# A hand-ordered attention, Hyena and conv-FFN kernel: earlier turns of probabilities, an output's turns between the third and fourth weighing, a net layer one gate tile later, and a few smaller reorderings

## The reference

```python
def first_block(x, ...):
    h = rms_norm(x, norm_in)
    (dq, dk, dv, dgate, cq, ckv, kr, mgate, g_diff, g_mla) = split(h @ w_in)
    # four differential heads: two causal softmaxes each, the second weighted by -lam
    o_diff = causal_multimap_attention(rope(dq), rope(dk), dv, [1, -lam], 64 ** -0.5)
    o_diff = rms_norm(o_diff, diff_subln) * (1 - lambda_init) * silu(dgate)
    # four latent heads: queries and keys from low-rank projections
    q = rms_norm(cq, mla_q_norm) @ w_uq;  kv = rms_norm(ckv, mla_kv_norm) @ w_ukv
    o_mla = causal_multimap_attention([q_nope, rope(q_rope)], [k_nope, rope(kr)], mv, [1], 192 ** -0.5)
    o_mla = o_mla * silu(mgate)
    merged = sigmoid(g_diff) * (o_diff @ w_proj_diff) + sigmoid(g_mla) * (o_mla @ w_proj_mla)
    return rms_norm(x + merged @ w_out, norm_final)

def second_block(x, c, ...):
    sh1, sc1, g1, sh2, sc2, g2 = adaln_params(c, mod_w, mod_b)     # the modulation
    x = x + g1 * hyena_mix(modulate(rmsnorm(x, norm_g[0]), sh1, sc1), p)   # its filter: a net of three
                                                   # small layers with sines, evaluated at all positions
    x = x + g2 * conv_ffn(modulate(rmsnorm(x, norm_g[1]), sh2, sc2), ...)
    return rmsnorm(x, final_g)
```

## Time and profile before

| | |
|---|---|
| time, median of 3 runs | 1042.02 us (1041.53 to 1042.57) |
| the profiled execution's own time | 1041.58 us |
| its span | 1039.4 us |
| PE busy | 1027.0 us (99%), 4886 matmuls |
| DVE busy | 738.0 us (71%) |
| POOL busy | 573.1 us (55%) |
| ACT busy | 413.7 us (40%) |
| mean DMA rate | 132 GB/s |

### The profile page before, as it was taken

One profiled execution on the slowest core, in us unless ns is written; L12 is line 12 of the kernel. 1 busy time (PEld: TensorE's weight loads), 2 busy tenths in 40 slices (PEclk: granted clock), 3 DMA queues, 4 the chain that ended last, 5 costly groups with the idle time before them and its releaser, 6 DMA issues.

```text
span 1039.4 us, 13302 instructions
## 1 busy us (share of the span) xinstructions
PE 1027.0 (99%) x4886; PEld 847.7 (82%) x4886; DVE 738.0 (71%) x1053; ACT 413.7 (40%) x681; POOL 573.1 (55%) x420
## 2 busy tenths in 40 slices
PE   9999999999999999999999999999999999999997
PEld 7889887777878888778888888778888888888886
DVE  7768957756878667994888968686666666671563
ACT  4233646665545244743444342533232223231222
POOL 2896996999410064545544276534655546574542
PEclk9999999999999999999999999999999999999999
DMA  8755364432665722404332223312222322223222
GB/s 343 289 199 201 117 212 148 107 137 92 212 172 198 295 109 81 162 14 108 123 122 81 102 84 145 117 65 98 81 81 81 135 107 81 81 81 128 115 81 81
DMA packets 21996, 136.91 MB, mean 132 GB/s; under 512 B 3973, under 2 KB 4405, under 8 KB 15288
## 3 DMA queue, kind: packets, MB, share of 16 engines
q1 hardware_dynamic: 9360, 94.74, 24.4%
q0 software_dynamic: 8224, 31.73, 9.9%
q10 hardware_dynamic: 4358, 9.72, 2.5%
HBM read 128.83 MB, written 6.31 MB: 130 GB/s over the span
## 4 chain that ended last, share of the span: by engine, by line
PE 83%; POOL 5%; DVE 5%; DMA 4%; ACT 2%; issue 1%; SPq 0%; ACTq 0%; POOLq 0%; DVEq 0%
PE bank L526 70%; PE bank L517 7%; DMA arena<-mod_w_in 4%; POOL arena L1819 2%; PE bank L532 2%; POOL arena L1817 1%; PE bank L787 1%; PE bank L781 1%; DVE ring_parts L2025 1%; DVE arena L2178 1%; DMA ring<-weights_in 1%; PE bank L776 1%; POOL mod_part L1822 0%; PE bank L997 0%; ACT ring_parts L1224 0%
## 5 line engine op out<-in xcount | busy, mean ns | idle before, releaser
L1801 POOL TENSOR_TENSOR ring_parts<-ring,ring_parts 128x1024 fp32r<-128x1024 f32 x101 | 251.6, 2497 | 237.7 <-ACT ring_parts L1224 234.1
L526 PE MATMUL bank<-hT_parts,ring_parts 128*128 128x512 f32 x1344 | 339.0, 393 | 1.2 <-ACT hT_parts L1567 1.2
L1224 ACT ACTIVATE ring_parts<-ring 128x1024 fp32r<-128x1024 f32 (+3 forms) x165 | 168.5, 1031 | 370.2 <-PE bank L526 172.6
L526 PEld LDWEIGHTS bank<-hT_parts,ring_parts 128*128 128x128 f32 x1344 | 249.6, 188 | 54.9 <-ACT hT_parts L1567 2.8
L526 PE MATMUL bank<-ring_parts,arena_parts 128*128 128x512 f32 (+1 forms) x744 | 172.9, 384 | 1.1 <-DVE ring_parts L2025 1.1
L526 PE MATMUL bank<-ring_parts,hT_parts 128*128 128x512 f32 (+2 forms) x676 | 168.3, 377 | 0.0
L526 PEld LDWEIGHTS bank<-ring_parts,arena_parts 128*128 128x128 f32 x744 | 137.4, 188 | 28.9 <-DVE ring_parts L2025 1.3
L526 PE MATMUL bank<-arena_parts,ring_parts 128*128 128x512 f32 x592 | 147.9, 390 | 0.0
L526 PEld LDWEIGHTS bank<-ring_parts,hT_parts 128*128 128x128 f32 x676 | 123.2, 188 | 21.0 <-issue 0.2
L2701 DVE SCALAR_TENSOR_TENSOR arena<-bank,small,arena 128x441 f32<-128x441 f32 (+2 forms) x176 | 122.3, 695 | 21.0 <-DVE arena L2701 1.4
L526 PEld LDWEIGHTS bank<-arena_parts,ring_parts 128*128 128x128 f32 x592 | 111.0, 188 | 24.7 <-DVE arena_parts L2458 2.0
(11 more groups left out here) (246 smaller groups left out, 1124.6 us busy)
## 6 DMA issues: line engine op xcount, KB each, us to landing
ring<-weights_in SPq DMA_DIRECT2D x39, 2048.0 KB, 7.9
arena<-mod_w_in POOLq DMA_DIRECT2D x32, 512.0 KB, 4.1
arena<-mod_w_in POOLq DMA_DIRECT2D x8, 1024.0 KB, 9.2
x_sb<-xT_in SPq DMA_DIRECT2D x4, 512.0 KB, 6.8
ring<-weights_in SPq DMA_DIRECT2D x4, 512.0 KB, 7.5
arena<-x_in SPq DMA_DIRECT2D x4, 512.0 KB, 11.0
mod_spill<-mod_part POOLq DMA_DIRECT2D x16, 128.0 KB, 2.2
arena<-mod_spill POOLq DMA_DIRECT2D x8, 256.0 KB, 4.2
```

The lines of the kernel that those rows point to most:

```text
L526: ins = nc.tensor.matmul(out, l, r, start=start and n == 0, stop=stop and n == len(passes) - 1)
L1224: return nc.scalar.activation(out, in_, ACT.Copy)
L1801: return nc.gpsimd.tensor_tensor(part(low), low, part(high), ALU.subtract)
```

## The change

What it does, in eight places:

1. **Early turns.** The first two turns of unit u's probabilities (`first_turns`) leave `values(u)` and go into `scores(u + 1)`: ahead of the masks in a differential unit, ahead of the third of four tiles in a latent one. In unit 0 the last part of the fill goes there too. Unit 7, which has no scores behind it, keeps its order.
2. **Outputs.** `turn_output(1)` to `turn_output(4)` move from behind the fourth weighing of units 3 to 6 to between the third and the fourth, in banks by a table.
3. **Roots.** The inverse roots of outputs are made one modulation chunk sooner on POOL.
4. **Net.** The second net layer comes behind gate tile 5 instead of 4, on TensorE, DVE and ScalarE; the fifth modulation chunk of DVE comes behind piece 12 instead of 13.
5. **Queries.** The last piece of UQ is split in two on DVE: columns 512 to 767 first, the rest behind two other operations.
6. **Fill 0** is cut otherwise: low parts of its first three pieces ahead of the scores of unit 1.
7. **ScalarE** splits the second piece of mgate behind the first copy of values.
8. **n2.** The first `input_full` of DVE comes ahead of the first `taps_ab`, and the other taps shift by a tile.

In the changed kernel the same code stands 2 to 26 lines further down.

```diff
--- before.py
+++ after.py
@@ -68,5 +68,5 @@
 MOD_EARLY = 3
-MOD_AFTER = (9, 13, 16, 17, 19)
+MOD_AFTER = (9, 12, 16, 17, 19)
 SGD_AFTER = 13
-ROOTS_AFTER = (10, 20, 22, 24, 26)
+ROOTS_AFTER = (10, 19, 21, 23, 25)
 PAUSE_AFTER = 16
@@ -126,3 +126,3 @@
 PIECE = SLOT // 4
-NET_AFTER = (2, 4, 7)
+NET_AFTER = (2, 5, 7)
 PIECES = 4
@@ -420,2 +420,4 @@
         FILL_BANK = (7, 5, 5, 5, 5, 5, 5, 3)
+        OUTPUT_BANK = (6, 1, 1, 1, 1, 6, 6, 6)
+        OUTPUT_AT = {3: 1, 4: 2, 5: 3, 6: 4}
 
@@ -704,3 +706,3 @@
                 for i in ((), (), range(KQ), range(KQ, KQ + KKV))[m]:
-                    take((i + 1) % 4, "lat_low", i + 1)
+                    take((i + 1) % 4, "lat_low", i + 1 + (i >= KQ))
                     turn((i + 1) % 4, [lat[:, t, i * P:(i + 1) * P] for t in range(TT)]).then_inc(sem("lat_turned"), 1)
@@ -724,4 +726,6 @@
                 if m == 0:
-                    pe.wait_ge(sem("piece_low"), FIRST_UQ + KQ)
+                    pe.wait_ge(sem("lat_low"), KQ + 1)
+                    pe.wait_ge(sem("piece_low"), FIRST_UQ + KQ - 1)
                 product3(bank[4 + m][:, 0:256], *pairs, start=False, terms=((0, 1),)).then_inc(sem("latq_done"), 1)
+            pe.wait_ge(sem("piece_low"), FIRST_UQ + KQ)
             for h in range(HEADS):
...
@@ -745,3 +749,3 @@
 
-            def scores(u):
+            def scores(u, between=None):
                 latent, h = u >= HEADS, u % HEADS
@@ -783,3 +787,5 @@
                             ins.then_inc(sem("half_scored"), 1)
-                for a, i in tiles:
+                for n, (a, i) in enumerate(tiles):
+                    if between and n == (2 if latent else 0):
+                        between()
                     out, q, keys = place(a, i)
@@ -790,3 +796,3 @@
 
-            def fill(u, qs=range(PIECES), last=True):
+            def fill(u, qs=range(PIECES), low_qs=range(PIECES)):
 
@@ -807,6 +813,8 @@
                         product3(bank[b], lefts[two], rights[two], start=q == 0, stop=False, terms=((0, 0), (1, 0)))
-                    if not last:
+                    if low_qs:
+                        pe.wait_ge(sem("piece_low"), FIRST_MGATE + low_qs[-1] + 1)
+                        ks = slice(2 * low_qs[0], 2 * low_qs[-1] + 2)
+                        ins = product3(bank[b], lefts[ks], rights[ks], start=False, stop=low_qs[-1] == PIECES - 1, terms=((0, 1),))
+                    if not low_qs or low_qs[-1] < PIECES - 1:
                         return
-                    pe.wait_ge(sem("piece_low"), FIRST_MGATE + 4)
-                    ins = product3(bank[b], lefts, rights, start=False, terms=((0, 1),))
                 else:
@@ -818,11 +826,20 @@
 
-            def values(u, between=None):
-                latent, h = u >= HEADS, u % HEADS
+            def turn_probs(u, i):
+                b = 5 + i % 2
                 p1 = probs1[u % 2]
+                pe.wait_ge(sem("probs_ready"), 4 * u + i + 1)
+                take(b, "pT_out", 4 * u + i + 1)
+                turn(b, [p1[:, OFF[i] + j * P:OFF[i] + (j + 1) * P] for j in range(i + 1)]).then_inc(sem("p_turned"), 1)
 
-                def turn_probs(i):
-                    b = 5 + i % 2
-                    pe.wait_ge(sem("probs_ready"), 4 * u + i + 1)
-                    take(b, "pT_out", 4 * u + i + 1)
-                    turn(b, [p1[:, OFF[i] + j * P:OFF[i] + (j + 1) * P] for j in range(i + 1)]).then_inc(sem("p_turned"), 1)
+            def turn_output(u):
+                pe.wait_ge(sem("o_ready"), u + 1)
+                take(OUTPUT_BANK[u], "oT_out", u + 1)
+                turn(OUTPUT_BANK[u], [o_tok[u % 2][:, m, :] for m in range(TT)]).then_inc(sem("o_turned"), 1)
+
+            def first_turns(u):
+                turn_probs(u, 0)
+                turn_probs(u, 1)
+
+            def values(u, between=None):
+                latent, h = u >= HEADS, u % HEADS
 
@@ -837,4 +854,2 @@
 
-                turn_probs(0)
-                turn_probs(1)
                 if between:
@@ -842,5 +857,5 @@
                 weigh(0)
-                turn_probs(2)
+                turn_probs(u, 2)
                 weigh(1)
-                turn_probs(3)
+                turn_probs(u, 3)
                 if between:
@@ -848,9 +863,6 @@
                 weigh(2)
+                if u in OUTPUT_AT:
+                    turn_output(OUTPUT_AT[u])
                 weigh(3)
 
-            def turn_output(u):
-                pe.wait_ge(sem("o_ready"), u + 1)
-                take(6, "oT_out", u + 1)
-                turn(6, [o_tok[u % 2][:, m, :] for m in range(TT)]).then_inc(sem("o_turned"), 1)
-
             def gate_tile(i, part=None):
@@ -877,3 +889,3 @@
                 if m == TT - 1:
-                    fill(0, range(PIECES - 1), last=False)
+                    fill(0, range(PIECES - 1), ())
                 tokens = slice(m * P, (m + 1) * P)
@@ -882,4 +894,9 @@
                          [two_parts(ukv[1], k, slice(0, 512)) for k in range(KKV)]).then_inc(sem("latk_done"), 1)
-            scores(1)
-            fill(0, (PIECES - 1,))
+            fill(0, (), range(PIECES - 1))
+
+            def rest_and_turns():
+                fill(0, (PIECES - 1,), (PIECES - 1,))
+                first_turns(0)
+
+            scores(1, rest_and_turns)
             values(0)
@@ -887,7 +904,8 @@
             for u in range(1, UNITS - 1):
-                scores(u + 1)
+                scores(u + 1, lambda: first_turns(u))
                 values(u)
-                if u >= 2:
-                    turn_output(u - 2)
+                if u == 2:
+                    turn_output(0)
                 fill(u + 1)
+            first_turns(UNITS - 1)
             values(UNITS - 1, lambda part: gate_tile(0, part))
...
@@ -1405,8 +1423,8 @@
                     wait("subln_ready", 1)
-                nc.scalar.activation(kT[:, u, :], bank[6], ACT.Identity, scale=st(SUBLN))
-                nc.scalar.activation(part(qT[:, u, :]), bank[6], ACT.Identity, scale=st(SUBLN)).then_inc(sem("oT_out"), 1)
+                nc.scalar.activation(kT[:, u, :], bank[OUTPUT_BANK[u]], ACT.Identity, scale=st(SUBLN))
+                nc.scalar.activation(part(qT[:, u, :]), bank[OUTPUT_BANK[u]], ACT.Identity, scale=st(SUBLN)).then_inc(sem("oT_out"), 1)
 
-            for m in range(2):
-                split_high(FIRST_MGATE + m)
+            split_high(FIRST_MGATE)
             mv_out(0)
+            split_high(FIRST_MGATE + 1)
             exps(0, (0,))
@@ -2181,2 +2199,9 @@
                 split_low(FIRST_UQ + k)
+
+            def split_last_uq(s):
+                p = FIRST_UQ + KQ - 1
+                wait("piece_high", p + 1)
+                low, high = piece_parts(p)
+                return V.tensor_tensor(part(low[:, s]), low[:, s], part(high[:, s]), ALU.subtract)
+
             for i in range(KQ + KKV):
@@ -2186,3 +2211,3 @@
                 if i == KQ:
-                    split_low(FIRST_UQ + KQ - 1)
+                    split_last_uq(slice(512, UQ_W)).then_inc(sem("lat_low"), 1)
                 wait("lat_out", i + 2 if i else 1)
@@ -2190,2 +2215,3 @@
                                        op0=ALU.mult, op1=ALU.subtract).then_inc(sem("lat_low"), 1)
+            split_last_uq(slice(0, 512)).then_inc(sem("piece_low"), 1)
             for m in range(TT):
@@ -2608,3 +2634,2 @@
             taps_even(0)
-            taps_ab(0, 0)
             wait("modc_ready", 1)
@@ -2613,6 +2638,6 @@
                 input_full("n2", 0, N2_BANKS, x_low, (k,))
-                if k == 0:
-                    taps_ab(0, 1)
-                if 2 <= k < 6:
-                    taps_cd(0, k - 2)
+                if k in (0, 2):
+                    taps_ab(0, k // 2)
+                if 3 <= k < 7:
+                    taps_cd(0, k - 3)
             add_abs(6)
```

8 lines of the change are left out of this document (4 added, 4 removed).

## The result

The changed kernel takes 1049.59 us (median of 4 runs, 1049.27 to 1050.77) against 1042.23 for the kernel before: ratio 1.0074, 95% interval 1.0061 to 1.0087. The forecast was 1045.1 with a range up to 1047.3, so the side was right and the size was not. The profiled run took 1049.27 us for a span of 1047.3.

The account below looks back on a forecast made before the run. TensorE, busy 99%, was taken as the bound. Gains of 5.0 us against 5.2 lost left 0.2 slower; with 2.9 for the clock, 1042.02 became 1045.1 us, range 1040.3 to 1047.3.

Parts of the forecast that it names:

- Net layer moved behind gate tile 5: Net stage: TensorE stands 5.7 us for ScalarE's late Sin, so the third net layer is 5.2 us late.
- The clock: Behind the net stage's stop TensorE's clock falls to half pace for 5.8 us, a loss of 2.9 us.
- Outputs turned between third and fourth weighing: Head loop, four units: an output's turns fill a 0.30 us stop before the fourth weighing; gain 1.15 us (0 to 1.2).
- the tie at 210.44 and 210.49: Unit 3: TensorE would ask for the output at 210.44, and it would be ready at 210.49.
- The sign that I had named: Head loop: TensorE waiting for probs_ready or o_ready would show the prediction wrong.
- Early turns: Units 1 to 6: masks cover ScalarE's copy between turns and first weighing; 0.42 us a unit, gain 2.5 us.
- The outputs of units 4 to 6: Head loop: turning each output before the fourth weighing removes a stop of 0.30 us a unit.
- UQ split: Last query piece: with 256 columns first, TensorE's wait of 1.10 us shrinks; gain 0.5 us (0.2 to 1.4).
- n2: At 439.92: VectorE's x_sb tile ahead of the tap lets TensorE's turn start 0.65 us sooner (0 to 0.8).
- Unit 0: First weighing: the early turn removes a 0.6 us wait, the third gate piece is 0.3 to 0.4 late; gain 0.2.
- The third rival: Head loop: late probabilities or outputs shrink 2.5 + 1.15 to 0; 1045.9 at full clock, 1048.8 with the fall; chance 0.10.
- the forecast: Net stage stop and fall of the clock behind it: 1045.1 us, chance 0.45.

Follow-up runs that it names:

- mod_back: Changed kernel with only the modulation chunk put back behind piece 13, the net layer left at gate tile 5: 1050.26 us, ratio 1.0077.
- mod_back_sin_first: As mod_back, with ScalarE's Sin of the second net layer also moved ahead of gate tile 6's split and sigmoid: 1041.46 us, ratio 0.9994.
- net_back: Changed kernel with the second net layer and the modulation chunk back at their old places: 1040.50 us, ratio 0.9989.
- outputs_back: Changed kernel with the net stage, GpSimd's roots and all four outputs' turns back at their old places: 1043.01 us, ratio 1.0007.
- outputs_back_new_roots: As outputs_back, but with GpSimd's roots at their new, sooner chunks: 1040.77 us, ratio 0.9989.
- net_back_u3: As net_back, with output 1 (unit 3's) turned behind the fourth weighing again: 1041.08 us, ratio 0.9994.
- pool_steps_aside: As net_back, with GpSimd held once, behind modulation chunk 22, until output 1 is ready: 1046.19 us, ratio 1.0039.
- aside_and_row: As pool_steps_aside, with GpSimd requesting the row of inverse roots ahead of its last modulation chunk: 1043.20 us, ratio 1.0008.

## Why the prediction was wrong

- **Net layer moved behind gate tile 5**: right. Stop 5.64 against 5.7 forecast, by the steps named. mod_back and mod_back_sin_first show that the cause, but for about a microsecond, is the Sin's place in ScalarE's list.
- **The clock**: right in direction, 2.3 us behind this stop (the difference grows from 6.16 to 8.45) against 2.9. The one fall in the earlier trace rows came 5.0 us behind the last matmul, and the step looked for no other; but the clock also went down behind the 2.6 us at 212 and cost 1.5 there (from +1.17 to +2.67; 1.6 against net_back). Stage and clock together cost 7.7 us (from +0.71 to +8.45), against 8.1.
- **Outputs turned between third and fourth weighing**: this is the step that failed. I had the tie at 210.44 and 210.49, priced it at nothing, and took the +1.15 gain, 0.3 of it in unit 3. I left out two things. The request came sooner by all that had been gained ahead of it (209.4, not 210.44), and the answer later (212.10, not 210.49), as the sooner roots put GpSimd's products beside VectorE's; outputs_back and outputs_back_new_roots, which differ in the roots alone, show 210.74 and 212.69. Measured in unit 3: 4.1 us lost (from -1.47 to +2.67), 2.6 of them the stop and 1.5 the clock, where 0.3 gained was forecast. These 4.4 us are about the whole miss (1049.6 less 1045.1); the errors in the other terms, below and above, go both ways and nearly cancel. The sign that I had named, a wait for o_ready in the head loop, is there. The new place of the turns alone did not do it: net_back_u3 with the old place still waits 1.4 us and is no faster. What made the output late is VectorE beside GpSimd, as pool_steps_aside shows.
- **Early turns**: a stop is gone in each unit, but it gave 0.29, 0.34, 0.26, 0.32 and 0.34 us at the first weighings of units 1, 2, 4, 5 and 6 (0.42 forecast), and in unit 3 TensorE lost 0.1, since the early turn found its bank not yet copied out (0.22). Sum 1.45 of 2.5. **The outputs of units 4 to 6** gave 0.33 each, as forecast (0.30). Both are real where they stand, and net_back, outputs_back and aside_and_row show how little of them is kept: waits for outputs of the first heads, late by VectorE beside GpSimd, and for the Sin ahead of the second net layer take it back. Of 3.65 us for both parts and 0.7 ahead of them, TensorE was 0.7 us late at 254.84. That TensorE is the bound was read from a busy share; one and a half microseconds sooner, it was no longer true.
- **UQ split**: 1.0 instead of 0.5. The 256 columns took 2.17 us beside a GpSimd product that started 0.6 sooner than before; the mechanism held (they ended 0.3 behind it), the place of GpSimd's product moved. **n2**: 0.6 against 0.65 (from +8.44 to +7.82). **Unit 0**: 0.2 lost instead of gained (-1.10 to -0.90 in the table); the third gate piece was late, as named, and took more than the early turn gave.
- The third rival (outputs late, clock falls, 1048.8) comes nearest, at a chance of 0.10, and I let the range leave it out. Its sum is not what happened, so its number is near in part by luck: it let the head loop's 3.65 us shrink to nothing, while 1.45 and three times 0.33 were there and one output cost 4.1. It and the forecast were not exclusive: each had a stop of its own.

## What to carry to other kernels

Where several edits each take a few tenths from the bounding engine, follow the engine behind it with the sum of them: find the first place where it delivers at a tie, and price that place at the sum, not at zero. An engine's order is only as good as what stands ahead of each result in its list: here one Sin that stood a gate tile too late in ScalarE's list cost 8.8 us. An edit on a third engine (the roots, the hold) changes which operations run beside each other and what waits for that engine further down; it is seen only in durations and releasers, row by row. And a profile is one execution: where the clock falls in some executions only, medians that differ by one or two microseconds can mix two cases.
